# Four more gate steps ahead of the latent norm's rows, and two gate stores asked for ahead of the last two modulation loads

## The reference, cut to what matters

```python
mod_x = silu(c) @ ada_w + ada_b                      # six modulation vectors of 1024
sh1, sc1, g1, sh2, sc2, g2 = split(mod_x, 6)
hx = modulate(rmsnorm(x, norm1_g), sh1, sc1)
fx, qlx, kvlx, krx, gx = split_proj(hx @ w_in)       # gx: 2048 gate columns
kx, vx = mla_kv(kvlx, krx, kv_norm_g, w_kvb, k_gain, rope)   # begins with rmsnorm(kvlx)
qx = mla_q(qlx, q_norm_g, w_qb, q_gain, rope)
g = sigmoid(gx + b_gate)
```

## Time and profile before

| | |
|---|---|
| Runs | 3058.37, 3061.62, 3062.98 us; median 3061.62 us |
| Profiled execution | span 3061.9 us from first to last instruction; no time other than the span is given for it |
| PE busy | 2942.3 us (96%) |
| DVE, ACT, POOL busy | 50%, 30%, 34% |
| Chain that ended last | PE 76%, DVE 10%, ACT 7%, issue 3% |
| DMA | 256.85 MB, mean 84 GB/s |

### The profile page before, as it was taken

The page is one execution under the profiler, slowest core; times in us unless marked ns, Lnnn a source line. Parts: engine busy times, 40 slices in busy tenths (PEclk is TensorE's granted clock), DMA queues, the critical chain, the costliest instruction groups (busy, mean ns, idle before and its releaser), DMA issues.

```text
span 3061.9 us, 37301 instructions
## 1 busy us (share of the span) xinstructions
PE 2942.3 (96%) x14926; PEld 2447.1 (80%) x14926; DVE 1516.5 (50%) x2288; ACT 923.1 (30%) x1606; POOL 1031.6 (34%) x454
## 2 busy tenths in 40 slices
PE   7999999999999999999999999998999999999997
PEld 3877778888887888888888878787888888887786
DVE  5843238887624313132244443555436666664545
ACT  5122326665113101010011112411335555553402
POOL 1333251000585434444444443242432121212241
PEclk9999999999999999999999999999999999999998
DMA  6534584221533111111111121111331212111111
GB/s 242 188 124 143 197 242 112 73 73 49 195 113 113 49 48 49 49 48 48 48 48 48 49 68 52 38 47 37 105 124 56 56 56 63 56 56 42 36 53 64
DMA packets 118090, 256.85 MB, mean 84 GB/s; under 512 B 47228, under 2 KB 69276, under 8 KB 113712
## 3 DMA queue, kind: packets, MB, share of 16 engines
q1 hardware_dynamic: 117936, 254.71, 25.7%
HBM read 210.20 MB, written 45.97 MB: 84 GB/s over the span
## 4 chain that ended last, share of the span: by engine, by line
PE 76%; DVE 10%; ACT 7%; issue 3%; DMA 1%; POOL 1%; SPq 0%; ACTq 0%; DVEq 0%; POOLq 0%
PE ps L428 23%; PE ps L430 22%; PE ps L429 22%; ACT tmp L1811 3%; PE ps L1285 2%; DVE tmp L3022 1%; PE ps L1273 1%; PE ps L1708 1%; DVE tmp L2545 1%; ACT Ea L1811 1%; PE ps L1694 1%; DVE Z L2323 1%; DVE mx L2774 1%; PE ps L1681 1%; PE ps L1680 1%
## 5 line engine op out<-in xcount | busy, mean ns | idle before, releaser
L844 POOL TENSOR_TENSOR whi<-raw,onesf 128x1024 fp32r<-128x1024 f32 x189 | 365.0, 1931 | 1901.5 <-PE ps L430 1777.4
L428 PE MATMUL ps<-Hb_hi,whi 128*128 128x512 f32 x1424 | 574.2, 403 | 10.3 <-DVE Y L2747 5.9
L430 PE MATMUL ps<-Hb_hi,wlo 128*128 128x512 f32 x1424 | 556.7, 391 | 0.0
L429 PE MATMUL ps<-Hb_lo,whi 128*128 128x512 f32 x1424 | 556.2, 391 | 0.0
L846 POOL TENSOR_TENSOR wlo<-raw,whi 128x1024 fp32r<-128x1024 f32 x189 | 504.1, 2667 | 14.9
L428 PEld LDWEIGHTS ps<-Hb_hi,whi 128*128 128x128 f32 x1424 | 268.6, 189 | 61.9 <-issue 8.1
L430 PEld LDWEIGHTS ps<-Hb_hi,wlo 128*128 128x128 f32 x1424 | 267.7, 188 | 57.7
L429 PEld LDWEIGHTS ps<-Hb_lo,whi 128*128 128x128 f32 x1424 | 268.7, 189 | 47.9
L1811 ACT ACTIVATE tmp<-ps 64x256 f32<-64x256 f32 (+2 forms) x97 | 57.7, 595 | 536.9 <-PE ps L430 465.1
L1811 ACT ACTIVATE tmp<-tmp,mx 128x1280 f32<-128x1280 f32 (+2 forms) x192 | 187.1, 974 | 65.0 <-DVE mx L3022 54.7
L429 PE MATMUL ps<-Ulo,whi 128*128 128x512 f32 x512 | 199.4, 389 | 0.0
(11 more groups left out here) (458 smaller groups left out, 5814.7 us busy)
## 6 DMA issues: line engine op xcount, KB each, us to landing
raw<-in_w SPq DMA_DIRECT2D x197, 512.0 KB, 3.5
adas<-in_ada SPq DMA_DIRECT2D x16, 1024.0 KB, 4.9
raw<-in_w SPq DMA_DIRECT2D x44, 256.0 KB, 3.9
adaE<-in_ada SPq DMA_DIRECT2D x4, 2048.0 KB, 23.2
gate_d<-gst SPq DMA_DIRECT2D x16, 512.0 KB, 2.8
v_d<-VS SPq DMA_DIRECT2D x2, 4096.0 KB, 14.9
ncB<-cum_d SPq DMA_DIRECT2D x16, 512.0 KB, 3.6
Vx<-v_d SPq DMA_DIRECT2D x16, 512.0 KB, 4.4
```

The lines of the kernel that those rows point to most:

```text
L428: nc.tensor.matmul(o, wh, xh, start=start, stop=False)
L429: nc.tensor.matmul(o, wh, xl, start=False, stop=False)
L430: return nc.tensor.matmul(o, wl, xh, start=False, stop=stop)
L844: nc.gpsimd.tensor_tensor(whi[b][:, 0:w], raw[b][:, 0:w], onesf[:, 0:1].to_broadcast([P, w]), ALU.mult).then_inc(S("split_hi"), 1)
```

## The change

`ROWS` goes from 22 to 26 and `COLUMNS` from 30 to 34; `STEP0` stays at 42. So `norm_rows` and `late_columns` come four gate steps later, and none of the four steps that stood between the last column sum's own step and `head_tile(0)` is left. In SP's queue the store of gate 0 comes ahead of the load of chunk 22; the store of gate 1 and the load of panel 5 come ahead of the load of chunk 23.

```diff
-SUMS, ROWS, COLUMNS, STEP0, STEPS = 10, 22, 30, 42, 5
+SUMS, ROWS, COLUMNS, STEP0, STEPS = 10, 26, 34, 42, 5
@@ sp_program
             if on("gates"):
                 load_panel("gates", 20, 0, 0)
-                for c in (22, 23):
+
+                def last_chunk(c):
                     sp.wait_ge(S("ada_used"), c - 9)
                     ada_chunk(c, c % 2)
@@
                     store_gate(t)
                     if t == 3:
                         rope_tables()
+                    if t == 0:
+                        last_chunk(22)
                     for j in {0: (), 1: (1, 2, 3), 7: (9, 10, 11)}.get(t, (gate_place(t),)):
                         load_panel("gates", 20, 0, j)
+                        if j == 1:
+                            last_chunk(23)
```

## The result

The changed kernel takes 3074.98 us (median of 6 runs, 3072.75 to 3079.71) where the kernel before takes 3062.30 in the same comparison (6 runs): +12.7 us, ratio 1.0041, 95% interval [1.0031, 1.0051]. The forecast was +9.7 us, 3071.3, and slower. One of the 11 runs of e6 was slow (6046.56 us), and its ratio leaves it out. The profiled execution has a span of 3073.6 us, 11.7 more than before.

A forecast was written before the change was run, and what follows sets the result against it. PE was taken to bound the kernel, busy for 2942.3 of 3061.9 us. Rows +2.6, wait before the square sums +5.4 and clock behind it +1.7 gave +9.7 us: 3061.62 to 3071.3 us, range 3065 to 3075.

The forecast's parts named there:

- The first wait: PE before the norm's rows (L967): 8.3 us where it waited 5.8; 7 to 9 us named as the sign.
- The second wait: PE before the first square sums (L1155): grows from 0.4 to 5.8 us; 5 to 6 us named as the sign.
- B: Rival: chunk 23 lands at 187 to 188, DVE sums it in 4 us without collision; +4.3 to +5.3 us, chance 0.20.
- C: Rival: chunk 23 still lands by about 184.5, PE waits 0.3 us at the rows; -1.2 us, 3060.4 us, chance 0.08.
- D: Rival: the key chain is released earlier, the square sums wait 0.4 us as before; +2.6 us alone, chance 0.04.
- E: Rival: both splits hit `qnlo` too, or a late panel shifts later splits; +13 to +17 us, chance 0.06.
- the seven instructions: DVE's seven L2347 on chunk 23, behind the last L2344: they would take 6 to 7 us.
- Rows at equal work: Start of the norm's rows, at equal work done by PE: later by 2.6 us, bounds -3.0 and +5.
- Clock behind the rows: PE's half clock after the wait at the norm's rows: about 5.4 us as before, no difference.
- Wait before the square sums: PE's wait there: +5.4 us as its cover shrinks by four steps, bounds 4.3 to 6.5.
- Clock behind it: PE at half clock after the wait before the square sums: +1.7 us, bounds 0 to 2.2.

The follow-up runs named there:

- e6: Changed kernel with COLUMNS 30 and chunk 23 ahead of the store of gate 1, panel 6's split not held: 3061.19 us against 3062.53, ratio 0.9994.
- e2: Changed kernel with ROWS 22 and COLUMNS 30, so only SP's new queue order is left: 3069.04 us, ratio 1.0021.
- e4: Changed kernel with POOL's split of panel 6 held until the latent norm's reciprocal is there: 3069.26 us against 3062.51, ratio 1.0025.
- e3: Changed kernel with COLUMNS back at 30, ROWS still 26: 3066.49 us against 3062.51, ratio 1.0013.
- e7: Kernel before with COLUMNS 34 alone, ROWS 22 and SP's old order: 3070.50 us against 3062.53, ratio 1.0024.
- e1: Kernel before with ROWS 26 and COLUMNS 34, SP's queue in the old order: 3070.37 us against 3062.51, ratio 1.0033.
- e9: e5 with panel 5 asked for directly behind panel 4 and ROWS 28: 3054.20 us against 3062.36, ratio 0.9975.
- e5: Changed kernel with COLUMNS 30, chunk 23 ahead of the store of gate 1, and panel 6's split held: 3059.94 us against 3062.53, ratio 0.9989.
- e10: e5 with panel 5 asked for directly behind panel 4, ROWS still 26: 3057.07 us, ratio 0.9986.
- e8: Changed kernel with COLUMNS 30 and panel 6's split held until the reciprocal: 3062.73 us against 3062.53, ratio 0.9998.

## Why the prediction was right

**Direction and both mechanisms** were as put. The first wait is not removed but lengthened, since the last chunk stands behind a store and a panel (shown by e2) and POOL's split of panel 6 then falls on DVE (shown by e4). The second wait comes from the steps that `STEP0` no longer leaves (shown by e3 and e7, in both directions). The rivals B (no collision), C (the wait goes) and D (no second wait) are out: the collision cost 3.7 us (7.29 against 3.61), the wait grew, and the second one is 6.6 us. So is E (both splits on `qnlo` too), though its +13 is near: the two `qnlo` begin at 198.69, behind both splits, and take 2.48 us as before. Three of the signs came out a little above what was named for them: the waits of 9.5 and 6.6 us (7 to 9 and 5 to 6), and the seven instructions with 7.29 us (6 to 7).

**The terms**, forecast and found in the profiled execution:

| Term | Forecast | Found |
|---|---|---|
| Rows at equal work | +2.6 | +3.7 |
| Clock behind the rows | 0 | -0.5 |
| Wait before the square sums | +5.4 | +6.2 |
| Clock behind it | +1.7 | +2.4 |
| Sum | +9.7 | +11.8 (span 11.7, medians 12.7) |

Three terms were each 0.7 to 1.1 us too small. *Rows:* panel 5 was in POOL's hands at 185.6, not at 184.9, so the chunk's first instruction ended at 190.15 and not at 189.6. By then panel 6's split was near (190.73): of the seven instructions behind the first, one was through before it and not three. The two that were held ended at 192.90 and 195.39, as forecast, but four were left behind them and not two, so the chunk was summed at 197.47 against 196.4. I had timed panel 5 by the best of the earlier trace rows, 4.6 us; it took 5.6. *Square sums:* I took the chain from the last column sum to the square as fixed at 16.8 us. It took 17.6 (235.1 to 252.7), because SP's fourteen small loads took longer to ask for: one of them, in SP's queue of the changed kernel, 1.26 us where its neighbours take 0.42.

```profile
239.71 0.42 SPq L573 DMA_DIRECT2D sinT<-in_sin  x1
240.19 1.26 SPq L574 DMA_DIRECT2D gains<-in_cols  x1
```

The same wait is 6.6 to 6.9 us in all four runs that have it (this one, e1, e4, e7), and the same load takes 1.26 to 1.44 us in each, so it belongs to the later place and is not chance; why it is so I did not test. *Clock:* half clock lasted 5.87 us, longer than either case that I had rows for. In e1, e4 and e7, behind the same wait, it lasted 3.2, 2.7 and 3.5 us, so +1.7 was a fair middle, and the 2.4 found is this execution's and not a fixed price of the wait.

The number landed at the upper edge of the range: 3074.98 us, where the range ends at 3075. That it lies inside is luck. The bounds of the terms were taken around my likeliest values, and three terms missed to the same side; the rows and the square sums stayed within their own bounds, the clock did not (2.4 against at most 2.2). One sum was off as well: B's lower end gives 3061.62 + 4.3 = 3065.9, not 3065.5.

**The Trainium skill's rule** on VectorE and GpSimd (SBUF — State Buffer, "Who interferes with whom"), that an instruction with two SBUF inputs and one of GpSimd that reads SBUF exclude each other, agrees: the seven instructions take 7.1 to 7.3 us when one split of 4.3 us falls in them (changed kernel, e9's chunk 22) and 3.61 when none does (e2, e4), and two `qnlo` take 4.89 instead of 2.48 (e5), while POOL's L850 beside them takes 3.20 instead of 2.4. That L2349, with one tile from SBUF and no second, was held until the split's end too (1.65 us instead of 0.35) goes with the same page's sentence on `tensor_scalar`, which counts it among the operations that can take both ports when their operands allow it.

## What to carry to other kernels

A step that is moved behind more cover must be followed to its consumers: here four steps were put ahead of one wait by taking them from between the next producer and its consumer, where they had hidden all but 0.5 us of a chain of 17 us. Where a queue is reordered so that a panel comes earlier, ask which load goes later, and on whose work the helper engine will fall when it handles that panel. The change moved the transfer on the critical chain and lost. The versions that gained left it first in the queue, and what they gained beyond 2.6 us came with moving the one transfer whose buffer had long been free.

## What was not expected of the hardware

The cost of PE's clock does not follow the length of the wait. The table gives, for the waits of PE in this stage, how long the granted clock stayed at 0.50 after PE had started again:

| Wait | Half clock behind it |
|---|---|
| 1.45 us (e10) | none |
| 3.6 us (e5, e6) | 2.9, 5.2 us |
| 5.6 to 5.9 us (before, e4, e7, e8) | 5.4, 5.4, 4.1, 3.5 us |
| 6.6 to 6.9 us (changed, e4, e7, and both of e1) | 5.9, 2.7, 3.5, 5.3, 3.2 us |
| 9.2 to 11.1 us (e3, changed, e2) | 4.4, 4.5, 5.7 us |

So each wait from 3.6 us on cost 1.4 to 2.9 us of work, and the same wait cost twice as much in one execution as in another. Closing the first wait from 5.6 to 1.45 us gave back the wait and also 2.1 us of the row matmuls, while lengthening it from 5.6 to 9.5 cost no more clock.
